# The first two query/key projections of layer 0 multiplied feature pair by feature pair, between the value projections

## What is computed

```python
ada = jax.nn.silu(c) @ w_ada[l] + b_ada[l]
sh1, sc1, g1, sh2, sc2, g2 = [a[:, None, :] for a in jnp.split(ada, 6, axis=-1)]
h = x * (1.0 + sc1) + sh1
...
qa, ka, va, qb, kb, vb = jnp.split(h @ w_in, AB_SPLITS, axis=-1)
...
s = jnp.einsum('bhmqd,bhmkd->bhmqk', qb, k).astype(f32) + bias_fn(q_pos)
```

## Time and the profile before

| | |
|---|---|
| median of 3 runs | 1231.93 us (1231.55 to 1232.69) |
| span of the profiled execution | 1231.6 us |
| PE busy | 1194.4 us (97%) |
| DVE busy | 674.5 us (55%) |
| ACT busy | 502.6 us (41%) |
| mean rate of the transfers | 321 GB/s |

### The profile page before, as it was taken

How to read it: one execution, slowest core, us unless ns; L and a number is a source line. 1 busy time by engine, 2 the same in 40 slices (tenths; PEclk the granted TensorE clock), 3 DMA queues, 4 the chain that set the end, 5 groups by cost and what they waited for, 6 DMA issues and landing times.

```text
span 1231.6 us, 16570 instructions
## 1 busy us (share of the span) xinstructions
PE 1194.4 (97%) x6586; PEld 822.9 (67%) x6586; DVE 674.5 (55%) x1222; ACT 502.6 (41%) x763; POOL 53.6 (4%) x103
## 2 busy tenths in 40 slices
PE   6899999999999999999999999999999999999997
PEld 2597678888889878888878776455444444554446
DVE  5599979887889787764476685112111121121126
ACT  1479663434565576344447384111112111111125
POOL 0100001000010000010001100000000000000000
PEclk9999999999999999999999999999999999999999
DMA  9996868887846555855567779999999999999990
GB/s 366 383 350 267 324 221 324 334 316 293 321 167 233 191 214 201 303 196 211 193 236 248 270 302 413 407 427 423 428 423 427 424 422 422 427 425 426 425 411 35
DMA packets 50987, 394.98 MB, mean 321 GB/s; under 512 B 6673, under 2 KB 8913, under 8 KB 11378
## 3 DMA queue, kind: packets, MB, share of 16 engines
q1 hardware_dynamic: 39618, 337.18, 68.4%
q0 software_dynamic: 9072, 53.92, 12.2%
q10 hardware_dynamic: 2240, 3.10, 0.9%
HBM read 390.68 MB, written 3.49 MB: 320 GB/s over the span
## 4 chain that ended last, share of the span: by engine, by line
PE 84%; DVE 8%; ACT 3%; DMA 3%; issue 1%; SPq 0%; DVEq 0%; ACTq 0%
PE psum L1400 18%; PE psum L770 10%; PE psum L773 10%; PE psum L777 10%; PE psum L1446 9%; PE psum L1332 5%; PE psum L1340 2%; PE psum L843 2%; PE psum L847 2%; PE psum L845 2%; DMA w_raw<-in_units 2%; DVE w_parts L2155 2%; PE psum L1095 1%; PE psum L804 1%; PE psum L1107 1%; PE psum L1086 1%
## 5 line engine op out<-in xcount | busy, mean ns | idle before, releaser
L2155 DVE TENSOR_TENSOR w_parts<-w_raw,w_parts 128x2048 fp32r<-128x2048 f32 x106 | 241.7, 2287 | 65.9 <-ACT w_parts L1536 65.8
L1536 ACT ACTIVATE w_parts<-w_raw 128x2048 fp32r<-128x2048 f32 x106 | 202.1, 1912 | 74.7 <-DMA w_raw<-in_units 74.7
L1400 PE MATMUL psum<-slabs,arena 128*64 128x512 f32 x768 | 222.5, 592 | 0.0
L770 PE MATMUL psum<-w_parts,h_parts 128*128 128x512 f32 x392 | 155.2, 396 | 3.9 <-DVE w_parts L2155 2.0
L773 PE MATMUL psum<-w_parts,h_parts 128*128 128x512 f32 x392 | 153.0, 390 | 0.0
L1400 PEld LDWEIGHTS psum<-slabs,arena 128*64 128x64 f32 x768 | 71.8, 137 | 109.2 <-issue 108.8
L1536 ACT ACTIVATE arena<-psum 128x512 f32<-128x512 f32 (+1 forms) x43 | 23.8, 556 | 243.7 <-PE psum L1419 140.0
L777 PE MATMUL psum<-w_parts,h_parts 128*128 128x512 f32 x392 | 105.3, 390 | 0.6 <-DVE h_parts L2333 0.6
L2138 DVE CUSTOM_DVE_ANT_0 aring<-aring,cb 128x1024 f32<-128x1024 f32 x80 | 94.5, 1219 | 0.7 <-DMA aring<-in_ada 0.6
L770 PEld LDWEIGHTS psum<-w_parts,h_parts 128*128 128x128 f32 x392 | 73.6, 188 | 20.5 <-issue 2.9
L1400 PE MATMUL psum<-w_odd,arena 128*64 128x512 f32 x192 | 85.0, 592 | 0.0
(11 more groups left out here) (341 smaller groups left out, 1907.7 us busy)
## 6 DMA issues: line engine op xcount, KB each, us to landing
w_raw<-in_units SPq DMA_DIRECT2D x110, 1024.0 KB, 5.0
slabs<-in_w SPq DMA_DIRECT2D x52, 1024.0 KB, 14.8
slabs<-in_w SPq DMA_DIRECT2D x22, 2048.0 KB, 20.6
aring<-in_ada POOLq DMA_DIRECT2D x40, 1024.0 KB, 5.4
arena<-in_w SPq DMA_DIRECT2D x16, 2048.0 KB, 19.3
w_odd<-in_w SPq DMA_DIRECT2D x16, 2048.0 KB, 19.6
w_odd<-in_w SPq DMA_DIRECT2D x24, 1024.0 KB, 24.7
staged<-in_ada SPq DMA_DIRECT2D x8, 1024.0 KB, 19.2
```

Of the source, the lines that this page charges most:

```text
L770: mm(psum[:, bank, :], high(tile, tok), w_hi(k)[:, col:col + 512], start=first and bank not in begun, stop=False, skip_group_check=True)
L1400: ins = nc.tensor.matmul(psum[s * CAP:(s + 1) * CAP, w, :], xe_t[:, kt, s * CAP:(s + 1) * CAP], up_weights(w, s, b, kt), start=kt == 0, st ...
L1536: return nc.scalar.activation(out_ap, in_ap, func, **kw)
L2155: v.tensor_tensor(w_lo(k), raw(k), w_hi(k).bitcast(F32), ALU.subtract).then_inc(w_split, 1)
```

## The change

Units 4 and 5 are laid out anew: unit 4 holds the first four feature tiles of the first 256 columns of queries and the first 256 of keys, unit 5 the other four feature tiles of the same 512 columns. A new function multiplies them a feature pair at a time:

```diff
+            def first_heads(i):
+                k = QK_AT + i // 2
+                weights(k)
+                pe.wait_ge(h_high, 2 * i + 2)
+                pe.wait_ge(h_low, 2 * i + 2)
+                for kt in (2 * i, 2 * i + 1):
+                    for j in range(2):
+                        for s in range(2):
...
+                            out_ = half(6 + j, s)
...
+                if i == 3:
+                    ins.then_inc(unit_done, 2)
```

PE's order (the unit loop of layer 0 then begins at `j == 2`), SP's order, and the places of the splits on ACT:

```diff
-                    for i in range(4):
-                        first_values(i)
+                    first_values(0)
+                    first_values(1)
+                    first_heads(0)
+                    first_heads(1)
+                    first_values(2)
+                    first_heads(2)
+                    first_values(3)
+                    first_heads(3)
...
-                for j in range(8):
+                for j in range(0 if layer else 2, 8):
...
                 load_unit(i)
-            load_unit(4)
+                if i in (1, 2):
+                    load_unit(QK_AT + i - 1)
...
-            for k in range(SLOTS, Z_AT):
+            for k in range(QK_AT + 2, Z_AT):
...
-            split(4)
+                if p in (1, 2):
+                    split(QK_AT + p - 1)
+            split(QK_AT + 2)
...
-                        split(u + 5 + t)
+                        if t == 0:
+                            split(u + QK_AT + 3)
...
-                    split(u + QK_AT + j + 3)
+                    if layer or j:
+                        split(u + QK_AT + j + 3)
```

On DVE the splits of units 4, 5 and 6 stand behind `first_low(1)`, `first_low(2)` and `first_low(3)`, and that of unit 7 behind the two small sums for lambda:

```diff
+            first_low(1)
+            split(QK_AT)
+            pieces(4, 6)
+            first_scale(2)
+            first_low(2)
+            split(QK_AT + 1)
+            pieces(6, 8)
+            first_scale(3)
             first_low(3)
-            split(4)
-            split(5)
+            split(QK_AT + 2)
```

More of the change, by code:

```diff
@@ L809, in first_values @@
                 ins.then_inc(unit_done, 1)
+            def first_heads(i):
[6 more added lines that the diff above has]
+                        for s in range(2):
+                            at_ = kt % 4 * 512 + j * 256 + s * P
+                            cols_ = slice(at_, at_ + P)
+                            out_ = half(6 + j, s)
+                            mm(out_, w_hi(k)[:, cols_], h_hi[:, kt, :], start=kt == 0 and s == 0, stop=False,
+                               skip_group_check=True)
+                            mm(out_, w_lo(k)[:, cols_], h_hi[:, kt, :], start=False, stop=False, skip_group_check=True)
+                            ins = mm(out_, w_hi(k)[:, cols_], h_lo[:, kt, :], start=False, stop=kt == KT - 1,
+                                     skip_group_check=True)
+                if i == 3:
+                    ins.then_inc(unit_done, 2)
             def to_values(i, t):
@@ L838, in to_heads @@
                         pe.wait_ge(v_taken, 4 * layer + j + 1)
+                    elif layer == 0 and j < 4:
+                        pe.wait_ge(v_taken, j - 1)
                     else:
@@ L1604, in take_qk @@
                 act.wait_ge(unit_done, LAYER_UNITS * layer + QK_AT + j + 1)
-                A(qk[:, tile:tile + 2, :].rearrange("p n t -> p (n t)"), psum[:, j % 2, :], Cp,
+                bank = j % 2 if layer or j >= 2 else 6 + j
+                A(qk[:, tile:tile + 2, :].rearrange("p n t -> p (n t)"), psum[:, bank, :], Cp,
                   scale=1.0 if is_k else -DH ** -0.5).then_inc(qk_taken, 1)
@@ L2202, in first_scale @@
             def first_scale(p):
-                pieces(2 * p, 2 * p + 2)
                 dve.wait_ge(ada_done, 2 * p + 2)
@@ L2212, in first_low @@
                                     ALU.subtract).then_inc(h_low, 1)
+            pieces(0, 2)
             first_scale(0)
-            for p in range(3):
-                first_scale(p + 1)
-                first_low(p)
-                if p == 0:
-                    dve.wait_ge(consts_in, CONSTS)
-                    dve.wait_ge(rows_mm, 2)
-                    stt(added_in[:], psum[0:16, 4, 0:384], -1.0, added_in[:], ALU.mult, ALU.add).then_inc(bias_row, 1)
+            piece(2)
+            first_low(0)
+            piece(3)
+            first_scale(1)
+            dve.wait_ge(consts_in, CONSTS)
+            dve.wait_ge(rows_mm, 2)
+            stt(added_in[:], psum[0:16, 4, 0:384], -1.0, added_in[:], ALU.mult, ALU.add).then_inc(bias_row, 1)
+            first_low(1)
[6 more added lines that the diff above has]
+            first_scale(3)
             first_low(3)
-            split(4)
-            split(5)
+            split(QK_AT + 2)
             dve.wait_ge(later_in, LATER)
@@ L2230, in _ @@
                                        accum_out=small[:, 10 + n:11 + n]).then_inc(lam_sum, 1)
-            split(6)
+            split(QK_AT + 3)
             def head_operands(pair):
@@ L2420, in _ @@
                         piece(8)
-                    if j == 0:
+                    if j == 0 and layer:
                         split(u + QK_AT + 3)
@@ L3047, in lay_out @@
         heads = col_units(np.concatenate([w[:, 0:1024], w[:, 1536:2560]], axis=1))
-        units += [heads[[0, 2, 1, 3, 4, 6, 5, 7]], row_units(f["w_o"][layer])]
+        if layer == 0:
+            first = np.concatenate([w[:, 0:256], w[:, 512:768]], axis=1)
+            units.append(first.reshape(2, 4, P, 512).transpose(0, 2, 1, 3).reshape(2, P, UNIT))
+        else:
+            units.append(heads[[0, 2]])
+        units += [heads[[1, 3, 4, 6, 5, 7]], row_units(f["w_o"][layer])]
         w_in, w_out = f["w_ffn_in"][layer], row_units(f["w_ffn_out"][layer])
```

## The result

The changed kernel is slower: a median of 1237.18 us in 5 executions (1236.52 to 1238.63), beside 1232.24 us (1231.55 to 1234.28) for the kernel before in the same comparison. The ratio is 1.0037, with a 95% interval of 1.0025 to 1.0049 (it is reckoned over the executions and isn't the quotient of the two medians). The forecast was 1234.7 (1231.6 to 1236.3): the sign is right, and the time lies 0.9 us above the range.

A forecast was written before the change was run, and what follows sets the result against it. PE was busy 97% of the span, its opening held by transfers. A 2.3 us lead would be lost and the scores start 2.8 us later: 1231.6 + 2.8 = 1234.4, median 0.33 higher, so 1234.7 us (range 1231.6 to 1236.3).

The forecast's parts named there:

- The mechanism: Opening: PE gains a 2.3 us lead, but unit 6 lands later and the first scores start 2.8 us later.
- ACT's order: Opening: high parts of units 6 and 7 precede ACT's query/key copies, 8.2 us from unit 6's landing to the copies' end.
- the rival of a delay taken up: Between 86.50 and 158 us: PE's and DVE's waits absorb the delay, 1232 to 1233.5 us; chance 15%.
- the rival of a lead kept: At the scores: PE's lead survives, unit 7 landing by 58.6, unit 6 by 55.7; 1230.9 or 1229.6 us; chance 12%.
- the sum's last line: Whole kernel: span 1231.6 + 2.8 = 1234.4; the runs' median lies 0.33 above the profiled span, so 1234.7 us.
- The absolute 66.7: First scores: start at 66.7 us, when ACT's copies of query and key are ready, 8.2 us after unit 6 lands.
- the distance of 2.8: First scores: start 2.8 us later than the 63.93 us in the profile of the kernel before.
- the rule that the forecast made of them: DMA engines: go round their queues a packet at a time, so small loads wait behind q0's 8 KB packets.
- the forward count: Unit 6's landing: from 48.4 us, adding band 0.6, pieces 5.0, small packets 1.3 and unit 6 2.5 gives 57.8.
- the backward bound: Unit 6's landing: unit 8 lands at 63.9 again with the same bytes, so unit 7 at 61.4, unit 6 at 58.9.
- the main case: First scores: start 2.8 us later through unit 6's late landing and ACT's order, 1234.7 us; chance 48%.
- the rival of more lost: Opening: unit 3 lands after 50, or DVE's 3.3 us reaches PE; 1236 to 1237 us; chance 8%.

The follow-up runs named there:

- `values_first`: Changed kernel with ACT making all copies before the high parts of units 6 to 8, and DVE lambda's sums before unit 6's low part: 1240.40 us, ratio 1.0064.
- `combo`: Changed kernel with most small loads behind unit 8, `w_ada` piece 9 held back, ACT's and DVE's orders changed: 1236.19 us, ratio 1.0028.
- `band_combo`: `combo` with GpSimd's band of biases also held back until DVE's last scale of the opening: 1234.97 us, ratio 1.0010.
- `ninth_late`: Changed kernel with GpSimd's load of `w_ada` piece 9 held back until ACT has made unit 7's high part: 1234.36 us, ratio 1.0011.
- `band_ninth`: `ninth_late` with GpSimd's band of biases also held back until DVE's last scale of the opening: 1232.57 us, ratio 0.9994.
- the two controls: Kernel before, once with `w_ada` piece 9 held back (1232.11 us, ratio 0.9988), once with four more zero matmuls in the router (1232.95 us, 0.9996).
- `warm`: Changed kernel with 44 unread matmuls filling PE's wait behind `first_heads(3)`: 1237.68 us, ratio 1.0036.
- `before_fill`: Kernel before with four more 128 x 512 zero matmuls between the router's steps: 1232.95 us, ratio 0.9996.
- `unit5_late`: Changed kernel with only unit 4 loaded ahead, unit 5 and its work back in their old places: 1241.12 us, ratio 1.0047.
- `small_late`: Changed kernel with five of the six small loads moved behind unit 8 on SP's queue: 1236.98 us, ratio 1.0036.
- `both`: Changed kernel with the edits of `warm` and `values_first` together: 1237.45 us, ratio 1.0034.
- `router_fill`: Changed kernel with four more 128 x 512 zero matmuls between the router's steps: 1236.62 us, ratio 1.0030.

## Why the prediction was right and wrong

**What held.** The mechanism, in this order: PE ends its first queries and keys earlier, the transfers behind aren't earlier, unit 6 is later, PE waits for its parts, and the lead is lost. Landings forecast and found: unit 6 58.5 and 58.1, unit 7 61.0 and 61.2; ACT's copies 66.7 and 66.6; first `shift` 68.6 and 68.8. ACT's order puts two high parts ahead of the copies, as forecast, but the sign given for it, PE waiting 1 us or more at the scores for the copies, isn't there in after, and the versions that turn the order around (`values_first`, `combo`, `band_combo`) gain nothing by it. None of the distance came back at 93 or 158, against the rival of a delay taken up (PE's idle time between 86.50 and 158, which the forecast counted as 8 us, is 6.4). And the rival of a lead kept fell as it was priced: it asked for unit 7 by 58.6 and unit 6 by 55.7. `ninth_late` comes near (58.5 and 56.1) and is level with before but for unit 3; `band_ninth` is past it and starts the scores ahead.

**The step that failed: the sum's last line, its base.** "The median of the runs lies 0.33 above this span" compared an execution with the median of others. In each of the 13 versions the device time of the profiled execution lies 1.6 us above its own span (1.58 to 1.66; 1238.3 and 1236.7 here), and so it does in all 78 executions of before that were timed with their span in the later comparisons (1.55 to 1.68). So the profile of before belongs to a time near 1233.2, not to one below the median. The table's column "rest" says what follows: every profiled execution without a late low-clock stretch has 1169.2 to 1169.6 us behind its first scores. That of before has 1233.2 - 63.9 = 1169.3, too, but its scores start 1.3 us later than in the two controls with the same order (62.59 and 62.60), because its opening began later (first value units at 15.08 and 14.61, and the later pieces of `w_ada` 0.8 to 0.9 later), and because unit 5 landed at 50.7, where the controls have 48.9 and 49.4, so that PE waited about 0.3 us for its parts. So I priced the change against an execution that was 1.3 us slow ahead of the scores. The absolute 66.7 was right; the distance of 2.8 is 4.1 against the controls. With 66.7 + 1169.4 the sum is 1236.1. Of the 2.5 us between the forecast and the median, 1.3 are this base.

**The term left out: TensorE's clock.** The sum let PE be ready "far earlier", its first half of unit 6 ending at 65.6. PE's start was right (62.7, found 62.45), but after 5.27 us without work the clock was at 0.50 and the half took 4.82 us instead of 2.88; it ended at 67.27, behind ACT's 66.6, and so PE and not ACT set the scores: 0.6 us more. The second stretch, at 760 us, is 1.6 us. 1236.1 + 0.6 + 1.6 = 1238.3, the time of this execution. The median is 1237.2 and the fastest 1236.5, the latter at a mean clock of 0.997; an execution without the second stretch would be at 1236.7.

**The small loads and unit 3.** The forecast had the small loads from 48.4 on, one packet in turn with each of q0's of 8 KB. In after they went mostly before that, 443 of their packets from 44 to 45 us with nothing of q0 beside them, and unit 3 landed at 46.8, not at 48.4, which it had by sharing the engines with the band all the way. Equal counts of packets of one size, as in the earlier trace rows, fit a share by bytes as well as one by packets, so they couldn't carry the rule that the forecast made of them. Both steps were wrong, and that unit 6 came within 0.4 of the forecast is luck as far as the forward count goes (57.8); the backward bound, by the bytes, is what carried the 58.5. What unit 6 shares the engines with is q0: piece 9 is worth 2.2 us of scores (64.42 in `ninth_late`, and 67.27 less the 0.6 of the clock in after). For unit 3 it is the band, where it is issued early.

**The range.** It ended at 1236.3; 1.3 us of base and 0.6 of clock more would have put the main case at 1236.6, outside it. It ended there since the rival of more lost had 8% and asked for unit 3 after 50. The clock wasn't in it at all: neither at PE's waits nor as something that differs from execution to execution.

**Open.** What brings the stretch at 760 us is open. It is in 5 of 14 profiles (after, `warm`, `values_first`, `combo`, `band_combo`), behind waits of 0.84 and 0.36 us that are the same in before, and never in one of the three of before's order. Five of the 11 with the changed order against none of three is not enough to tie it to the change, and `before_fill` kept executions of 1233.8 to 1239.3 without showing one. Open too is what moves the band's issue between 38.9 and 41.5 us, and with it unit 3's landing between 46.5 and 49.7, and what the slower executions of `unit5_late` and `band_ninth` do.

## What to carry to other kernels

A unit moved ahead gives PE a lead only as long as the next transfers keep up with it: forecast the landing behind the gap, ask which queue's bytes are in front, and move those that nobody waits for yet (here holding back 1 MB on GpSimd's queue took the ratio from 1.0037 to 1.0011). A transfer issued on another engine's signal can come 2.6 us earlier or later from one execution to the next (the band, 38.85 to 41.46), and what it collides with changes with it. A wait of 2.5 to 5 us that a change opens on PE isn't free beyond its length, since the matmuls behind it may run at the half clock; cost it at both levels. Before a profile is compared with a median, put its execution beside others by one landmark (the start of the first scores), or take the unknown, here 1.3 us, into the range.

## What the runs showed of the hardware

- The granted clock fell to 0.50 in stretches of 3.4 or 6.8 us in or up to 0.9 us behind PE's waits of 2.5 to 5.3 us in the opening (`band_combo` 2.5, `combo` at unit 6 2.5, `small_late` 2.75, `both` 3.1, `router_fill` 3.3, `ninth_late` 3.8, `combo` at unit 3 4.1, after and `values_first` 5.3), and not at waits of 1.1 to 1.9 (`band_combo`, after, `router_fill`, `band_ninth`, before), 2.2 (`warm`) or 2.3 (`unit5_late`). In `small_late` it fell a second time, behind a wait of 2.0, and at 760 us behind 0.84 and 0.36.
- Two queues in one stretch, q0 to q1: 226 to 220 packets with 8 KB packets on both the earlier trace rows, 104 to 201 with the band and the small loads (`warm`, 45 to 47 us).
- GpSimd's band was issued from 41.07 us on in after, and its queue moved no byte before 45 us.
- With 0.55 MB in 179 packets on GpSimd's queue, most of it a band of biases, the 16 engines moved 280 GB/s in 44 to 50 us, and 401 without it (`ninth_late`, `band_ninth`).
- The device time of an execution lay 1.55 to 1.68 us above its span, in every execution that has both.
- Executions of one kernel spread by 2 to 10 us, the slower ones mostly at a lower mean granted clock (`unit5_late`: 1232.4 at 0.999, 1242.1 at 0.993), but not by it alone (before: 1233.11 at 0.997, 1239.82 at 0.996).
